# Last expert layer: seven weight slots in place of three, four of them in working buffers; output weights of the recurrent layer loaded in its readout

## The reference

```python
# recurrent mixer, its end: y is normalized per head, a bonus term times v is added, then gated and projected
o = (group_norm(y) * ln_g + ln_b + bonus * v) * (sigmoid_lora(h) @ g2)
xl = xl + gt1 * (o @ w_o)                       # w_o: 1024 x 1024
# experts: every expert picks its 64 best of the 512 tokens (EC_CAPACITY * 512 / 16)
hl = modulate(rms_norm_2(xl, norm2_g), sh2, sc2)
xl = xl + gt2 * expert_choice_ffn(hl, router, w1, w3, w2)
# expert_choice_ffn: for each of 16 experts, on its 64 tokens:
#   out += affinity * ((silu(x @ w1) * (x @ w3)) @ w2)     w1, w3, w2: 1024 x 1024 each
```

## Time and profile before

| | |
|---|---|
| median of three runs | 3702.89 us |
| the profiled execution, in all | 3688.93 us |
| its span | 3687.2 us |
| PE busy | 3203.8 us, 87% of the span |
| DVE busy | 1534.7 us, 42% |
| ACT, POOL busy | 820.9 us, 277.9 us |
| DMA | 605.43 MB, mean 164 GB/s |
| the last experts' stage | from 3144 us to the end |

### The profile page before, as it was taken

The page is one execution under the profiler, slowest core; times in us unless marked ns, Lnnn a source line. Parts: engine busy times, 40 slices in busy tenths (PEclk is TensorE's granted clock), DMA queues, the critical chain, the costliest instruction groups (busy, mean ns, idle before and its releaser), DMA issues. The chain is left out here.

```text
span 3687.2 us, 73003 instructions
## 1 busy us (share of the span) xinstructions
PE 3203.8 (87%) x32020; PEld 1845.8 (50%) x32020; DVE 1534.7 (42%) x3500; ACT 820.9 (22%) x1780; POOL 277.9 (8%) x265
## 2 busy tenths in 40 slices
PE   6997999989799899699999889978888867678787
PEld 5844558555344564344444344557777753222222
DVE  4565436644212572422222253167777753211111
ACT  2114211143201570100000010056655530000000
POOL 0000000000000110000000000001222220000000
PEclk9998899998899999799999989979999988899999
DMA  6663135610221102599999920100000013799998
GB/s 178 164 200 110 24 99 149 212 46 24 93 78 39 33 26 91 199 373 373 375 366 378 342 81 23 40 26 4 4 4 4 4 50 141 277 398 402 398 397 342
DMA packets 147238, 605.43 MB, mean 164 GB/s; under 512 B 17264, under 2 KB 20144, under 8 KB 129904
## 3 DMA queue, kind: packets, MB, share of 16 engines
q1 hardware_dynamic: 140592, 579.19, 42.9%
q0 software_dynamic: 6336, 21.63, 2.5%
HBM read 576.00 MB, written 31.07 MB: 165 GB/s over the span
## 5 line engine op out<-in xcount | busy, mean ns | idle before, releaser
L1750 PE MATMUL psum<-ring,big 128*64 128x512 f32 (+1 forms) x6144 | 906.9, 502 | 106.1 <-DMA ring<-moe_w 53.7
L1750 PEld LDWEIGHTS psum<-ring,big 128*64 128x64 f32 (+1 forms) x6144 | 305.6, 126 | 687.2 <-issue 524.2
L1888 DVE TENSOR_TENSOR big<-big,psum 128x512 f32<-128x512 f32 (+1 forms) x48 | 27.3, 597 | 637.2 <-PE psum L1750 637.2
L391 PE MATMUL psum<-h_uT,ring 128*128 128x264 f32 x1280 | 290.5, 387 | 0.0
L520 DVE SCALAR_TENSOR_TENSOR h_O<-h_O,cond_silu 128x512 f32<-128x512 f32 x336 | 226.7, 744 | 100.0 <-DMA h_O<-ada_w 100.0
L391 PEld LDWEIGHTS psum<-h_uT,ring 128*128 128x128 f32 x1280 | 242.0, 190 | 46.5 <-issue 5.8
L1235 PE MATMUL psum<-ring,big 128*128 128x512 f32 x576 | 249.4, 592 | 1.7 <-PEq L55 1.7
L2328 PE MATMUL psum<-ring,gates 64*64 64x128 f32 (+1 forms) x5120 | 171.7, 256 | 78.0 <-ACT ring L2511 72.0
L2328 PEld LDWEIGHTS psum<-ring,gates 64*64 64x64 f32 x5120 | 134.7, 134 | 93.5 <-DVE ring L2669 83.9
L1900 DVE SCALAR_TENSOR_TENSOR big<-psum,big,gates 64x512 f32<-64x512 f32 (+1 forms) x128 | 78.8, 615 | 237.5 <-PE psum L1750 236.1
L1235 PEld LDWEIGHTS psum<-ring,big 128*128 128x128 f32 x576 | 108.4, 190 | 133.5 <-issue 133.5
(11 more groups left out here) (343 smaller groups left out, 4483.1 us busy)
## 6 DMA issues: line engine op xcount, KB each, us to landing
ring<-moe_w SPq DMA_DIRECT2D x192, 2048.0 KB, 10.3
h_O<-ada_w SPq DMA_DIRECT2D x192, 256.0 KB, 3.0
ring<-w_in SPq DMA_DIRECT2D x16, 2048.0 KB, 13.0
ring<-na_w_qkv SPq DMA_DIRECT2D x6, 2048.0 KB, 8.1
ring<-w_out SPq DMA_DIRECT2D x4, 2048.0 KB, 8.6
bias_rows<-na_table SPq DMA_DIRECT2D x16, 480.0 KB, 15.6
ring<-bias_rows SPq DMA_DIRECT2D x16, 360.0 KB, 3.0
rows<-big SPq DMA_DIRECT2D x10, 512.0 KB, 4.4
```

The lines of the kernel that those rows point to most:

```text
L391: last = nc.tensor.matmul(bank(k, pair_bank(q) + h, NH), w[:, a, f * P:(f + 1) * P], uT[:, a, halves[h]], start=a == 0, stop=a == KD - 1)
L1750: last = nc.tensor.matmul(bank(k, b, r.width)[q * r.n:(q + 1) * r.n, :], rowsT[:, half * HALF_K + n, r.first:r.first + r.n], w[:, n, q * r ...
```

## The change

Seven slots: from the first chunk of the last experts on (`k.wide_from`), chunks go round seven slots: the ring's three, and the first 4096 of the 6144 elements per partition of C, E, B and A, in this order. The experts' working tiles of that layer move into the remaining 2048 elements of each of the four buffers. Chunks 3 and 4 of the experts are loaded at the start of `add_projection` (into C and E), chunk 5 in `route` behind PE's last use of B, chunk 6 behind the stores of A; in `experts` a load is issued when the chunk seven places before it has been used. `hold` is gone: its three loads are issued at the start of the readout, w_o 0 ahead of the load of X and the other two behind it. In the readout, PE turns V of pairs 0 to 3 first, and the gates follow V by four places; ACT copies gates out two steps later.

```diff
+WIDE_SLOTS = SLOTS + 4
+def chunk_slot(k, c):
+    n = (c - k.wide_from) % WIDE_SLOTS
+    return c % SLOTS if c < k.wide_from else (k.wide_from + n) % SLOTS if n < SLOTS else n
+
+def slot_tile(k, slot):
+    if slot < SLOTS:
+        return k.ring[:, slot]
+    A, B, C, E = k.big
+    flat = (C, E, B, A)[slot - SLOTS][:, :, :].rearrange("p a b -> p (a b)")
+    return flat[:, 0:KD * CHUNK].rearrange("p (a b) -> p a b", a=KD)
+
 def load_chunk(k, sp, c):
-    slot = c % SLOTS
+    slot = chunk_slot(k, c)
     for place, src in k.chunks[c]:
-        sp.dma_start(place(k.ring[:, slot]), src).then_inc(k.chunk_loaded[slot], 16)
+        sp.dma_start(place(slot_tile(k, slot)), src).then_inc(k.chunk_loaded[slot], 16)
...
@@ route, SP
             for t, _ in tiles:
                 sp.dma_start(sums[t * P:(t + 1) * P, :], k.X[:, t, :]).then_inc(k.sums_stored, 16)
+            if k.c == k.wide_from:
+                sp.wait_ge(s.parts, len(streams))
+                load_chunk(k, sp, k.c + SLOTS + 2)
+                sp.wait_ge(k.rows_stored, k.n_stored + 16 * nt)
+                load_chunk(k, sp, k.c + SLOTS + 3)
@@ experts
-def experts(k, l, aff, slot, sums, room_a, room_b, with_ctx):
+def experts(k, l, aff, slot, sums, rooms, with_ctx):
...
+        depth = SLOTS if with_ctx else WIDE_SLOTS
...
             for e in range(EXPERTS):
                 for j in range(W_CHUNKS):
-                    c = c0 + e * W_CHUNKS + j + SLOTS
+                    c = c0 + e * W_CHUNKS + j + depth
...
-                n = (c0 + j) % SLOTS
-                pe.wait_ge(k.chunk_loaded[n], e * (16 * W_CHUNKS // SLOTS) + loaded0[n] + 16 * (j // SLOTS + 1))
-                return half_rows(k.ring[:, n])
+                return half_rows(chunk_here(k, pe, c0 + e * W_CHUNKS + j))
@@ expert_layer
-        experts(k, l, aff, slot, sums, C, E, with_ctx)
+        flat = lambda buf: buf[:, :, :].rearrange("p a b -> p (a b)")
+        rooms = [flat(C), flat(E)] if with_ctx else [flat(buf)[:, KD * CHUNK:] for buf in (A, B, C, E)]
+        experts(k, l, aff, slot, sums, rooms, with_ctx)
@@ rwkv_readout
             sp.dma_start(g2, k.d["rw_g2_2"][0]).then_inc(s.g2_here, 16)
-            sp.dma_start(k.X[:, 0:LT, :], k.x_saved).then_inc(s.restored, 16)
+            for c in range(k.c, k.c + 3):
+                if c == k.c + 1:
+                    sp.dma_start(k.X[:, 0:LT, :], k.x_saved).then_inc(s.restored, 16)
+                if c + SLOTS < len(k.chunks):
+                    load_chunk(k, sp, c + SLOTS)
             sp.wait_ge(s.restored, 16)
...
-            for p in range(PAIRS):
-                pe.wait_ge(s.shaded, p + 1)
-                if p >= QUAD:
-                    pe.wait_ge(s.v_out, p - QUAD + 1)
-                turned(V, p % QUAD, p, p >= QUAD).then_inc(s.v_turned, 1)
-                if p == 0:
-                    pe.wait_ge(s.g2_here, 16)
+            def make_gate(p):
                 if p >= QUAD:
                     pe.wait_ge(s.gate_out, p - QUAD + 1)
                 nc.tensor.matmul(bank(k, QUAD + p % QUAD), g2[:, p * P:(p + 1) * P], tg[:, :], start=True, stop=True).then_inc(s.gate_made, 1)
+            for p in range(QUAD):
+                pe.wait_ge(s.shaded, p + 1)
+                turned(V, p, p, False).then_inc(s.v_turned, 1)
+            pe.wait_ge(s.g2_here, 16)
+            for p in range(QUAD, PAIRS):
+                make_gate(p - QUAD)
+                pe.wait_ge(s.shaded, p + 1)
+                pe.wait_ge(s.v_out, p - QUAD + 1)
+                turned(V, p % QUAD, p, True).then_inc(s.v_turned, 1)
+            for p in range(QUAD, PAIRS):
+                make_gate(p)
...
-                act.wait_ge(s.gate_made, n + 1)
-                nc.scalar.activation(gate(n), bank(k, QUAD + n % QUAD), ACT.Copy).then_inc(s.gate_out, 1)
+                if n >= 2:
+                    gate_out(n - 2)
             root(n_chunk - 1)
+            for p in range(PAIRS - 2, PAIRS):
+                gate_out(p)
@@ rwkv_layer
-    hold(k)
-    add_projection(k, mixT, TILES2[:LT], k.X, lambda t: k.gates[:, 0, :])
+    add_projection(k, mixT, TILES2[:LT], k.X, lambda t: k.gates[:, 0, :], held=[k.wide_from + SLOTS, k.wide_from + SLOTS + 1])
```

More of the change, by code:

```diff
@@ L67, in __call__, with chunk_total @@
         self.eng.wait_ge(self.sem, self.base + self.n)
+def chunk_slot(k, c):
[7 more added lines that the diff above has]
+    return flat[:, 0:KD * CHUNK].rearrange("p (a b) -> p a b", a=KD)
+def chunk_total(k, c):
+    return 16 * sum(len(k.chunks[x]) for x in range(c + 1) if chunk_slot(k, x) == chunk_slot(k, c))
 def load_chunk(k, sp, c):
-    slot = c % SLOTS
+    slot = chunk_slot(k, c)
     for place, src in k.chunks[c]:
-        sp.dma_start(place(k.ring[:, slot]), src).then_inc(k.chunk_loaded[slot], 16)
+        sp.dma_start(place(slot_tile(k, slot)), src).then_inc(k.chunk_loaded[slot], 16)
 def feed(k, sp, c0, product, ends):
@@ L87, in chunk_here @@
 def chunk_here(k, pe, c):
-    total = 16 * sum(len(k.chunks[x]) for x in range(c % SLOTS, c + 1, SLOTS))
-    pe.wait_ge(k.chunk_loaded[c % SLOTS], total)
-    return k.ring[:, c % SLOTS]
+    slot = chunk_slot(k, c)
+    pe.wait_ge(k.chunk_loaded[slot], chunk_total(k, c))
+    return slot_tile(k, slot)
 def columns(w, n):
@@ L1660, in experts, with carve @@
     wide = lambda r: slice(r.at * streams[0].width, r.at * streams[0].width + r.width)
[L1661 to L1665, removed]
+    used = [0] * len(rooms)
+    def carve(n, *dims):
+        first, used[n] = used[n], used[n] + math.prod(dims)
+        assert used[n] <= rooms[n].shape[1]
         letters = "abcd"[:len(dims)]
         pat = f"p ({' '.join(letters)}) -> p {' '.join(letters)}"
[L1668 to L1680, removed]
+        return rooms[n][:, first:used[n]].rearrange(pat, **dict(zip(letters, dims)))
+    more = 0 if with_ctx else 2
+    onehot, xinT = carve(more, 2, nt, P), carve(more, 2, KD, M)
+    xg, y = carve(0 if more else 1, 2, D), carve(1, 2, D)
+    pair, gate, hidT = carve(more + more // 2, 2, nt, 2), carve(more + more // 2, ROUND, 4), carve(more + more // 2, KD, M)
+    hid, silu, labels = carve(more + 1, W), carve(more + 1, W), carve(more + 1, 2 * P + LT + CT)
     iota = labels[:, 0:2 * P].rearrange("p (x m) -> p x m", x=2)
     token_id = labels[:, 2 * P:2 * P + nt]
-    assert at <= (LT + CT) * D
     INDEX_AT = HALF_K * M
@@ L1688, in experts @@
         index = mem.enter_context(nc.sbuf_tensor(f"index{k.stage_no}", [P, ROUND], mybir.dt.int32))
-        loaded0 = [16 * sum(len(k.chunks[x]) for x in range(n, c0, SLOTS)) for n in range(SLOTS)]
+        depth = SLOTS if with_ctx else WIDE_SLOTS
         @block.sync
@@ L2815, in root, with gate_out @@
                 nc.scalar.activation(stat[:, 1, c, :], stat[:, 1, c, :], ACT.Sqrt, bias=64e-5, scale=1.0 / CH).then_inc(s.rooted, 1)
+            def gate_out(p):
+                act.wait_ge(s.gate_made, p + 1)
+                nc.scalar.activation(gate(p), bank(k, QUAD + p % QUAD), ACT.Copy).then_inc(s.gate_out, 1)
             for n in range(n_chunk):
@@ L2862, in _ @@
                     nc.vector.tensor_tensor(mixT[:, p, :], term(p), gate(p), ALU.mult)
[L2865 to L2872, removed]
     k.c += 3
@@ L2973, in build @@
     k.chunks = weight_chunks(d, layers)
+    k.wide_from = len(k.chunks) - EXPERTS * W_CHUNKS if "moe1" in layers else len(k.chunks)
     k.bias_rows = nc.dram_tensor("bias_rows", [NA_HEADS, P, COPY], F32).ap()
@@ L2989, in build @@
         k.X = mem.enter_context(nc.sbuf_tensor("X", [P, LT + CT, D], F32))
-        k.chunk_loaded = [nc.alloc_semaphore(f"chunk_loaded{n}") for n in range(SLOTS)]
+        k.chunk_loaded = [nc.alloc_semaphore(f"chunk_loaded{n}") for n in range(WIDE_SLOTS)]
         always = resident(k, mem, RESIDENT)
```

## The result

The changed kernel takes 3669.57 us, the median of four runs (3665.29 to 3672.58), against 3702.07 for the kernel before in four runs (3694.21 to 3703.06). The ratio is 0.9916, 95% interval 0.9899 to 0.9933: 32.5 us less by the medians. The forecast of 3673.5 is 4 us off and the time lies in its range.

A forecast was written before the change was run, and what follows sets the result against it. The last experts' stage was taken as bound by the DMA engines, with a second loss at the readout's end. Terms 19.6 + 8.0 + 0 + 1.8 = 29.4 us, against the 3702.89 median, gave 3673.5 us, range 3661 to 3685.

The forecast's parts named there:

- Seven slots, 19.6 us: Last experts' stage: 89 chunks left to load, not 93; four chunks at 4.89 us save 19.6 us, bounds 15.2 and 21.9.
- Output weights, 8.0 us: End of the readout: with the three loads issued at its start, PE starts the projection at 3035.79, not 3043.78; gain 8.0 us.
- The clock at the projection, 0: Projection's start: PE's slow clock after idling costs about 2 us; gain taken as 0, with 2 us as upper bound.
- V ahead of gates, 1.8 us: Readout: square 1, the table load and the first root come 1.8 us earlier; gain 1.8 us, bounds 0 and 2.8.
- Where the loads go: Chunks 3 and 4 fit in the projection, 5 and 6 in the router's stage, over near 3136 us; cost 0, at most 10.
- Scatters behind a deeper queue: Rival, experts' stage: scatters wait behind six loads; landings beyond 33.0 us cost 16 us per us, 3722 at 36; chance 0.03.
- A slower stream: Rival, experts' stage: more outstanding loads cut the rate by 4 to 5%, leaving 9.8 us of 19.6, 3693 us; chance 0.06.
- a faster one: Rival, experts' stage: more outstanding loads shrink the loss to gathers and scatters, say by half, 3646 us; chance 0.05.
- the 55 us: Experts' stage: 93 chunks at 4.89 us are 455 of 510 us; the other 55 go to gathers and scatters, not removed.
- Loads in the way: Rival, router's stage: loads 5 and 6 are in the way of stores and labels, 10 us, 3683 us; chance 0.05.
- catch up with the stream after 24 chunks: Experts' stage: PE, at 24.3 us per expert against 33.0 for DMA, runs ahead and never waits until about 24 chunks in.
- a wait before chunk 20: Sign of error, experts' stage: PE waiting before chunk 20; the first wait for a weight was expected 25 to 35 chunks in.

The follow-up runs named there:

- the second experiment: The changed kernel with the last experts on the ring's three slots again, the rest kept: 3688.14 us, ratio 0.9973, 17.5 us over the changed kernel measured beside it.
- the run with 16 rows: The changed kernel with each last-layer scatter writing 16 of its expert's 64 rows, the other 48 left out: 3653.33 us, ratio 0.9876.

## Why the prediction was right

The stretches of the traces, each from its own start, in us ("to the projection" is from the readout's end to PE's first matmul of the projection):

| | readout | to the projection | first load of the experts to the last chunk |
|---|---|---|---|
| before | 38.22 | 8.78 | 512.6 |
| changed, four traces with seven slots and the preload | 35.5, 35.5, 35.5, 38.2 (gate after each V) | 0.82, 0.83, 0.82, 8.68 (hold back) | 489.3, 492.5, 490.0, 489.9 |
| three slots; seven without preload | 35.5, 35.5 | 0.82, 0.82 | 507.7; 510.5 |
| nine slots, twice | 35.5, 35.5 | 0.82, 0.82 | 481.3, 481.2 |

*Seven slots, 19.6 us: right, in size too.* With three slots the stretch takes 510.1 us on average (two traces), with seven 490.4, with nine 481.3. That is 4.9 us per chunk for the first four and 4.6 for the next two, where the forecast had 4.89 from the windows with weights alone and rejected the stage's mean of 5.48. The medians of the second experiment say 17.5. The reason given for it also held: gathers and scatters are not removed with the chunks. By these averages the 23.3 us of the first pair of traces were one long and one short execution. That the engines stay the bound, at an unchanged rate, is shown by the windows; that it is the preload and not the depth, by the run without it.

That the forecast came within 0.1 us of the averages is partly luck. Its price of a chunk is from windows of 4 and 6 us, and others of the same stage, as short, show anything from 401 to 455 GB/s:

```profile
3196.00:3200.00 4.00, 2.14 (x12) 0.64 (x12) 0.00 (x0) 0.60 (x1) 0.00 (x0) 1.00 1.03 442
3231.00:3236.00 5.00, 3.65 (x16) 1.06 (x16) 0.00 (x0) 0.00 (x0) 0.00 (x0) 1.00 0.95 401
3230.00:3234.00 4.00, 2.67 (x14) 0.96 (x16) 0.00 (x0) 0.21 (x1) 0.00 (x0) 1.00 1.06 455
```

By these four chunks would be 18.4 to 20.9 us. From three to nine slots the stretch shrinks by 28.9 us for six chunks, 4.8 us each, 435 GB/s. The Trainium skill, "DMA: Bandwidth & Descriptors", section Bandwidth, puts the ceiling of the 16 engines' ports at 435. The traces agree with that, but with 3 us of spread the 28.9 us allow anything from some 395 to 485 GB/s.

*Output weights, 8.0 us: right.* 8.78 - 0.82 = 7.96 by the traces, 7.86 with `hold` put back.

*The clock at the projection, 0: right.* PE sat idle 11.9 us ahead of the projection before, and 4.67 us now, and both were followed by a granted clock of 0.50 from 3044 to 3046 us, back at 1.00 by 3048. Beside the earlier trace rows, the changed kernel's row:

```profile
3044.00:3046.00 2.00, 2.00 (x3) 0.67 (x2) 0.00 (x0) 0.00 (x0) 0.00 (x0) 0.50 0.80 246
```

The 128 matmuls took 56.99 us before and 56.87 after, and from PE's start on them to the router's first store it is 72.11 and 72.00 us; the traces of the experiments have 70.6 to 71.6 for it.

*V ahead of gates, 1.8 us: the mechanism right, the term too small.* The first reciprocal gained 1.89 us, as worked out. The readout gained 2.67 (2.62 when undone). The missing 0.8 is what the forecast had kept as a bound: the gates made later keep PE busy nearer to Y's turn, 1.25 us of idle PE in place of 3.75, and Y's turn then runs at the full clock and takes 7.68 us in place of 9.23. The clock inside Y's turn, first in the changed kernel and then in the run with a gate after each V:

```profile
3032.00:3034.00 2.00, 2.00 (x76) 2.00 (x73) 1.36 (x2) 0.00 (x0) 0.71 (x1) 1.00 0.00 0
3036.00:3038.00 2.00, 2.00 (x48) 2.00 (x43) 0.75 (x1) 0.00 (x0) 0.53 (x1) 0.52 0.00 0
```

*Where the loads go: right.* Chunks 5 and 6 keep the engines busy to about 3138 us, where 3136 was forecast, and the labels are asked for at 3143.93. The labels took 2.03 us to land, 2.11 before, and the stretch from the router's first store to the experts' first matmul of a chunk was 41.08 us, 41.18 before. The first stores, before and then after:

```profile
3115.89 2.88 SPq L1562 DMA_DIRECT2D rows<-big  x4
3115.61 2.87 SPq L1581 DMA_DIRECT2D rows<-big  x4
```

The experiments say the same: 39.4, 39.5 and 39.4 us in three runs with chunks 5 and 6 in that stage, 39.5 and 39.9 in the two without them. (The traces of before, after and `hold` back have 41.1 to 41.3, with or without the loads. In them the router's first sixteen matmuls take 3.3 to 3.5 us, in the others 1.9.)

*The rivals.* Scatters behind a deeper queue: the landing time of line 1744 is unchanged, beside the earlier trace rows:

```profile
DMA to landing us min/median/max: 4.6/9.2/10.7
```

This line, like that of the earlier trace rows, counts the sixteen scatters of the layer before as well. The last layer's sixteen alone land in 9.3 us by the median in both kernels, 10.4 at most before and 10.5 after. So the queue of POOL gets its turn beside six loads as beside two. The rule of the Trainium skill named there ("DMA: Bandwidth & Descriptors", Queues, rings and completion order) agrees with this. A slower stream would have shown some 380 GB/s, a faster one, with half of the 55 us gone, some 420; it is 399, for 398 before. (Both are estimates from the rates and terms of the forecast.) Loads in the way would have shown at the labels, and by the numbers above they don't.

*One step was wrong.* I had PE catch up with the stream after 24 chunks, and called a wait before chunk 20 a sign of error. It came at chunk 17, so by my own sign this step failed:

```profile
3221.49 3.65 PE L1765 MATMUL psum<-ring,big 128*64 128x512 f32 x16
3225.60 3.65 PE L1765 MATMUL psum<-big 128*64 128x512 f32 x16 [0.46 <-DMA big<-moe_w]
```

That row is chunk 17, the last of the third expert; PE computes 0 to 16 without a wait for a load. I had let PE and the stream start together with PE seven chunks of loading ahead, 34 us. But the stream's first load is issued 5.3 us after PE's first matmul, and its bytes flow some 2 us later still. And a PE that doesn't wait between chunks is faster than 3.65 us each: 48 matmuls, three chunks, take 10.5 us in the same timeline. That makes 3.9 us per chunk with the turns and lists between, against 5.5 for the stream, and by these (34 - 7) / 1.6 = 17, an estimate made with the answer known. The time doesn't hang on it, since DMA bounds the stage either way.

The sum of 29.4 us stands against 34.0 in one pair of traces and 32.5 and 29 in medians. By the averages of the stretches it is 19.7 + 8.0 + 2.7 = 30.4. Each of the three parts was undone by a run of its own; for the third only the trace shows it, since it is smaller than the spread of the medians.

## What to carry to other kernels

Where a stage is bound by its loads, a deeper ring was worth the chunks that were already there when the stage began, at about the rate that the engines reach with those bytes alone; look for dead buffers and idle DMA time just ahead of it, and expect no more once the idle time is full (here nine slots all but fill it). Undo the preload alone to see that it isn't the depth. And compare stretches from an instant of their own, since spans of unchanged work can differ by more than the change is worth.

## What was not expected

*The issue of a load can block SP.* With up to seven loads outstanding, SP took up to 15.7 us to issue one:

```profile
L95 SPq DMA_DIRECT2D ring<-moe_w x138: 327/341/15601, 1394.7 to 3608.3; - x138
L95 SPq DMA_DIRECT2D big<-moe_w x54: 328/1171/15719, 3043.6 to 3618.6; - x54
```

(The numbers are the shortest, the median and the longest issue in ns.) The number of loads outstanding is what makes it: in this stage no issue took over 0.38 us before, nor with three slots in the otherwise changed kernel,

```profile
L95 SPq DMA_DIRECT2D ring<-moe_w x93: 327/340/379, 3166.1 to 3662.5; - x93
```

while without the preload seven slots have up to 16.4 us and nine slots up to 20.6. A few loads in a row are enough for a part of it: the third load of `hold` took 3.20 us to issue, and the one behind four others in the changed readout 6.74. It costs nothing here, as SP has nothing else to do and the share stays at 1.01. A store or a small load behind such an issue on SP would have had to wait for it; no run here has one.

*An accumulating scatter's byte costs about two of the weights'.* 4.5 us per MB by the run with 16 rows (4.2 to 5.3 with the spread) against 4.8 / 2.097 = 2.3 for weights, 2.097 MB being a chunk. Even so, the fifteen scatters in the stretch, 3.93 MB, are then some 18 us of it and the fifteen gathers, as many bytes priced as weights, 9 more, an estimate from these prices. The forecast left 55 us to both. What the other half is stays open: contention beside gathers, or windows of pure weights that are too favourable; no run here parts these.

*The spread of unchanged work.* The instant at which the readout starts moved over 25 us between traces of kernels that are the same up to there, while the readout itself repeated within 0.05 us. The differences are there already in the first layers: the last load of `w_in` is issued at 672.0 us in the trace of before and at 681.7 in that of after. Their cause wasn't looked for.
